# Attention scores of two maps in alternating products on separate row groups, for B and C two heads together in every other step

## The chip, the cores and the metric

The kernel runs on one core of one Trainium2 chip. The metric is the device time in microseconds (us) of one execution.

## What is computed

One inference step of a two-layer model with 128 context tokens and 512 latent tokens (640 together), width 1024. Each layer normalises, projects, runs four branches (A differential attention, B neighbourhood attention, C latent attention, D a convolution), gates and merges them, and ends in a mixture of experts. The change touches the scores of branches A, B and C only. Cut to what matters:

```
# A: 4 heads, two maps each, 32 columns a map; B and C: 4 heads each, one map of 64 columns
s = einsum('bqhmd,bkhmd->bhmqk', q, k) * scale          # A
w = softmax(s)[:, :, 0] - lam * softmax(s)[:, :, 1];  o = w @ v
p = softmax(q @ k.T * scale (+ bias and mask in B));  o = p @ v      # B, C
```

A latent token attends to 128 cached and 512 own keys (640), a context token to its own 128.

## The kernel before, in words

It is written engine by engine, with semaphores by hand. All products are made of fp16 halves: an fp32 operand is split in a high and a low part, and `passes` (L413) issues three matmuls, high by high, high by low, low by high, into one PSUM area.

Attention is one stage in each layer. Queries are taken in five tiles of 128 tokens: four latent tiles first, the context tile last (`ORDER`). A tile has twelve heads: 0 to 3 are A's with two maps each, 4 to 7 are B's, 8 to 11 C's, one map each, so 16 maps (`MAPS`). `head(g)` gives the tile, head and maps of the global head number g. Each engine walks over the steps g and does, in this order, a part for several heads:

- TensorE (L1036 to L1057): the scores of head g+1 (`score`), at tile boundaries six transposes of finished outputs (L1047), `turn` of head g-1 (five fp32 transposes of the weights into the PSUM area `pr(2)`, L1021), `values` of head g-2 (15 small matmuls), and then the step's share of the gate projection, in sets of three matmuls of 320 columns (`gate_set`): eight sets in steps whose next head is one of A's, four in the others (`quota`). The gate sets fill TensorE while the other engines work.
- ScalarE (L1480 to L1535): the scaled output of head g-3 (L1487), the exponentials of head g (L1502), the gate's tanh (L1414) where a gate tile has ended, the high half of the turned weights of head g-1 (L1524, "the cast"), and conversions of gate weights (L1341).
- VectorE (L2112 to L2180): the low half of the turned weights of head g-2 (L2117, "the subtraction"), then for head g+1 the bias (B alone, L2127) and the row maximum (L2130), then the reciprocal of head g's sums (L2145), for A the mixing of two maps (L2155). In the step of head g-2 = 5 it also takes the variance of A's outputs (L2164 to L2168), at g-2 = 7 it scales them (L2172 to L2177).

`pr(2)`, into which `turn` writes, is a single buffer: `turn` waits with `pt_ready` until the subtraction of the head before is done. A score goes to `pr(0)` or `pr(1)`, by the parity of its map (banks 0 and 1, or 2 and 3), and waits with `ex_ready` until the exponential two maps earlier has read it.

A's maps lie 32 rows apart in `qThi` and `kThi` (rows 0, 32, 64 or 96), B's and C's 64 rows apart (rows 0 or 64). A map's score is two pieces, of 128 and of 512 keys (`SEG`), with three matmuls each.

Of the kernel before, what the change touches and what calls it, by code (L numbers as in the profile page):

```python
# [16 lines left out]
P = 128  # L17
# [4 lines left out]
TOK = CTX + LAT  # L22
# [46 lines left out]
MAPS = 16  # L69
# [13 lines left out]
def build(nc, t):  # L83
    ctx = ExitStack()
    with ctx:
# [3 lines left out]
        def sig(name, per_layer=0, before=0):  # L89
            return Signal(ctx.enter_context(nc.semaphore(name)), per_layer, before)  # L90
# [62 lines left out]
        kThi = ab[:, AR:AR + 4608].rearrange("p (c k) -> p c k", c=6)  # L153
        kTlo = ab[:, AR + 4608:AR + 9216].rearrange("p (c k) -> p c k", c=6)
        vhi = ab[:, AR + 9216:AR + 13824].rearrange("p (c k) -> p c k", c=6)
        vlo = ab[:, AR + 13824:AR + 18432].rearrange("p (c k) -> p c k", c=6)
        qThi = ab[:, AR + 18432:AR + 22272].rearrange("p (c k) -> p c k", c=6)
        qTlo = ab[:, AR + 22272:AR + 26112].rearrange("p (c k) -> p c k", c=6)
# [116 lines left out]
        def pr(pair):  # L275
            return PS[:, pair, 384:1024]
# [3 lines left out]
        def bank(n, w=512):  # L280
            return PS[:, n // 2, 512 * (n % 2):512 * (n % 2) + w]
# [72 lines left out]
        s_done = sig("s_done", TILES * MAPS)  # L354
        mx_ready = sig("mx_ready", TILES * MAPS)
        ex_ready = sig("ex_ready", TILES * MAPS)
# [56 lines left out]
        def passes(pe, out, st_hi, st_lo, mv_hi, mv_lo, first, last):  # L413

            for n, (st, mv) in enumerate(((st_hi, mv_hi), (st_hi, mv_lo), (st_lo, mv_hi))):
                ins = pe.matmul(out, st, mv, start=first and n == 0, stop=last and n == 2)  # L416
            return ins

        def passes640(pe, pair, st_hi, st_lo, mv_hi, mv_lo, first, last):

            for n, (st, mv) in enumerate(((st_hi, mv_hi), (st_hi, mv_lo), (st_lo, mv_hi))):
                for a, b in SEG:
                    ins = pe.matmul(pr(pair)[:, a:b], st, mv[:, a:b], start=first and n == 0, stop=last and n == 2)  # L423
            return ins

        def ran_before(eng):


            b, ran = (eng.value_load(loopi[0:1, n:n + 1], min_val=0, max_val=LAYERS * (PAIRS + 1)) for n in (0, 2))
            return b, ran, b + ran  # L430
# [12 lines left out]
        def head(g):  # L443

            if not 0 <= g < HEADS_ALL:
                return None
            ti, hd = divmod(g, HDS)
            return ti, ORDER[ti], hd, ((2 * hd, 2 * hd + 1) if hd < 4 else (hd + 4,))
# [309 lines left out]
        def _(pe):  # L758

            pe.wait_ge(*consts_in(0, 5 * 16))  # L760
            for tile in range(TILES):
# [3 lines left out]
                for k in range(KC):  # L765
                    ins = pe.transpose(PS[:, tile % 4, k * P:(k + 1) * P], xtok[:, tile, k * P:(k + 1) * P], ident[:, :])
# [98 lines left out]
            for l in range(LAYERS):  # L865
# [3 lines left out]
                for u in range(2):  # L869
                    pe.wait_ge(*w_lo(l, V_IN + u + 1))  # L870
                    for c in range(2):
                        for k in range(KC):
                            if u == 0 and c == 0:
                                pe.wait_ge(*h_ready(l, k + 1))
                            w = slice(k * 256 + c * P, k * 256 + (c + 1) * P)
                            ins = passes640(pe, 2 * u + c, whi[u][:, w], wlo[u][:, w], hhi[:, k, :], hlo[:, k, :],
                                            k == 0, k == KC - 1)
                        ins.then_inc(du_done.sem, 1)

                for u in range(2, IN_UNITS):  # L880
                    n = 256 if u < IN_UNITS - 1 else 160
                    pe.wait_ge(*w_lo(l, V_IN + u + 1))
                    for tile in range(TILES):
                        g = (u - 2) * TILES + tile
                        if g == LN_MEAN:
# [3 lines left out]
                            for (a, b), z0 in zip(SEG, (0, CTX + PAD)):  # L889
                                for c in range(2):  # L890
                                    ins = pe.matmul(pr(0)[:, a:b], ones[:, :], zacc[:, c, z0:z0 + b - a],
                                                    start=c == 0, stop=c == 1)
                            ins.then_inc(mu_done.sem, 1)
                        if g == LN_VAR:

                            pe.wait_ge(*proj_ready(l, g - 2))
                            for c in range(2):
                                pe.wait_ge(*zsq_ready(l, c + 1))
                                for a, b in SEG:
                                    ins = pe.matmul(pr(2)[:, a:b], ones[:, :], zsg[:, c, a:b], start=c == 0, stop=c == 1)  # L900
# [9 lines left out]
                        for k in range(KC):  # L910
                            ins = passes(pe, bank(g % 6, n), hhi[:, k, tile * P:(tile + 1) * P],
                                         hlo[:, k, tile * P:(tile + 1) * P], whi[u % 2][:, k * n:(k + 1) * n],
                                         wlo[u % 2][:, k * n:(k + 1) * n], k == 0, k == KC - 1)
# [28 lines left out]
                for n in range(TILES + 2):  # L942
                    own = n < TILES
                    if n <= TILES:
# [5 lines left out]
                        for c in range(0 if own else 2, 3):  # L950
                            src = cn[:, c * P:(c + 1) * P] if own else cache[:, 1024:1152]
                            ins = pe.transpose(bank(0)[:, c * P:(c + 1) * P], src, ident[:, :])
# [6 lines left out]
                        for c in range(4):  # L959
                            ins = pe.transpose(bank(4 + 2 * (n % 2))[:, c * P:(c + 1) * P], src[:, c * P:(c + 1) * P],  # L960
                                               ident[:, :])
                        ins.then_inc(ab_t.sem, 1)
                    if own:
                        if n:
                            pe.wait_ge(*ab_ready(l, 2 * n))
                        for c in range(4):
                            ins = pe.transpose(bank(5)[:, c * P:(c + 1) * P],
                                               proj[:, n, C_BQ + c * P:C_BQ + (c + 1) * P], ident[:, :])
                        ins.then_inc(ab_t.sem, 1)
                    gate(2 * n)  # L970
                    if n:
# [4 lines left out]
                        for c in range(0 if n <= TILES else 2, 4):  # L976
                            ins = pe.transpose(bank(3)[:, c * P:(c + 1) * P], qkc[:, c * P:(c + 1) * P], ident[:, :])
# [14 lines left out]
                pe.wait_ge(*c_ready(l, 6))  # L992
                pe.wait_ge(*v_ready(l, 1))

                def score(ti, tile, m):

                    if ti or m >= 2:
                        pe.wait_ge(*ex_ready(l, ti * MAPS + m - 1))
                    if m < 8:
                        lo, n, c = 32 * (m % 4), 32, m // 4  # L1000
                    else:
                        lo, n, c = 64 * (m % 2), 64, (m - 8) // 2 + 2
                    q = (slice(lo, lo + n), c, slice(tile * P, (tile + 1) * P))
                    for a, b in SEG if tile else SEG[:1]:
                        k = (slice(lo, lo + n), c, slice(a, b) if tile else slice(TOK, TOK + P))
                        ins = passes(pe, pr(m % 2)[:, a:b], qThi[q], qTlo[q], kThi[k], kTlo[k], True, True)
                    ins.then_inc(s_done.sem, 1)

                def turn(ti, tile, hd):

# [13 lines left out]
                def values(ti, tile, hd):  # L1024

                    pe.wait_ge(*pt_ready(l, ti * HDS + hd + 1))
                    if ti or hd:
                        pe.wait_ge(*o_ready(l, ti * HDS + hd))
                    kts = range(TILES) if tile else (5,)
                    for c, kt in enumerate(kts):  # L1030
                        ins = passes(pe, bank(6, 64), pthi[:, hd % 2, c * P:(c + 1) * P],
                                     ptlo[:, hd % 2, c * P:(c + 1) * P], vhi[:, kt, hd * 64:(hd + 1) * 64],
                                     vlo[:, kt, hd * 64:(hd + 1) * 64], c == 0, c == len(kts) - 1)
                    ins.then_inc(pv_done.sem, 1)

                for g in range(-1, HEADS_ALL + 4):  # L1036
                    if head(g + 1):
                        for m in head(g + 1)[3]:
                            score(*head(g + 1)[:2], m)
                    if head(g - 4) and head(g - 4)[2] == HDS - 1:  # L1040

                        ti = head(g - 4)[0]
                        pe.wait_ge(*o_ready(l, (ti + 1) * HDS))
                        pe.wait_ge(*on_ready(l, ti + 1))
                        pe.wait_ge(*pt_ready(l, min(g - 1, HEADS_ALL)))
                        for c in range(6):
                            ins = pe.transpose(PS[:, 2, c * P:(c + 1) * P], otok[:, ti % 2, c * P:(c + 1) * P], ident[:, :])  # L1047
                        ins.then_inc(ot_done.sem, 1)
                    early = 4 if head(g - 4) and head(g - 4)[2] == HDS - 1 and head(g - 1) else 0
                    for i in GATE_SETS[g][:early]:  # L1050
                        gate_set(i)
                    if head(g - 1):
                        turn(*head(g - 1)[:3])
                    if head(g - 2):
                        values(*head(g - 2)[:3])
                    for i in GATE_SETS[g][early:]:
                        gate_set(i)  # L1057

# [4 lines left out]
                for d in range(KC):  # L1063
                    for n, b in enumerate(SLOTS):
# [13 lines left out]
                        for k in range(2):  # L1078
                            w = slice(d * P, (d + 1) * P)
                            ins = passes640(pe, n, wohi[:, b, k, w], wolo[:, b, k, w], bhi[k], blo[k], k == 0, k == 1)  # L1080
# [3 lines left out]
                for u in range(OUT_UNITS):  # L1084
                    pe.wait_ge(*w_lo(l, V_OUT + u + 1))
                    for c in range(2):
                        d = 2 * u + c
                        pe.wait_ge(*x1_ready(l, d - 1))
                        for k in range(KC):
                            if d == 0:  # L1090
# [3 lines left out]
                            ins = passes640(pe, c, whi[u % 2][:, w], wlo[u % 2][:, w], mhi[:, k, :], mlo[:, k, :],  # L1094
                                            k == 0, k == KC - 1)
# [8 lines left out]
                for k in range(KC):  # L1104
                    pe.wait_ge(*hf_ready(l, KC + k + 1))
                    pe.wait_ge(*wr_in(l, 4 * 16))
                    for a, b in SEG:
                        ins = pe.matmul(pr(2)[0:20, a:b], wr[:, k, :], hf[:, k % 2, a:b], start=k == 0, stop=k == KC - 1)
                    if k >= 2:
                        pe.wait_ge(*htk_ready(l, k - 1))  # L1110
                    for tile in range(TILES):
                        ins = pe.transpose(pr(k % 2)[:, tile * P:(tile + 1) * P], hf[:, k % 2, tile * P:(tile + 1) * P],
                                           ident[:, :])
                    ins.then_inc(hf_used.sem, 1)
                pe.wait_ge(*lg_ready(l, 1))
                for tile in range(TILES):
                    ins = pe.matmul(bank(4)[:, tile * 20:(tile + 1) * 20], lgT[:, tile * P:(tile + 1) * P],
                                    ident[0:20, 0:20], start=True, stop=True)
# [13 lines left out]
                for n in range(10):  # L1132
                    ins = pe.matmul(bank(5)[:, 0:CHUNKS + 2], rowhot[:, n, :], chhot[:, n, :], start=n == 0, stop=n == 9)
# [7 lines left out]
                b, ran, past = ran_before(pe)  # L1141
# [53 lines left out]
                with pe.Fori(0, p + 1) as i:  # L1195
                    for n in range(2):

                        c, j = i * 2 + (1 + n), 1 - n
# [1352 lines left out]
```

## Time and profile before

| what | value |
|---|---|
| median of 3 runs | 1963.04 us (1955.48 to 1973.32) |
| the profiled execution's own time | 1951.89 us |
| its span, first to last instruction | 1950.0 us |
| TensorE busy | 1724.3 us, 88% |
| VectorE, ScalarE, GpSimd busy | 1149.6, 936.8, 439.9 us |
| mean granted TensorE clock | 0.93 |
| attention in the first layer | from 305 to 589 us of the span |

The second layer's attention runs from about 1247 to 1531 us. "Busy" is the time in which an engine had an instruction in work; the granted clock is a share of 2.4 GHz.

### The profile page before, as it was taken

To read this page: it belongs to the slowest core of one execution; us is meant where nothing else is said; L and a number is where in the kernel's file an instruction comes from. 1 tells how busy PE (TensorE), PEld (TensorE's weight loads), DVE (VectorE), ACT (ScalarE), POOL (GpSimd) and SP (SyncE) were. 2 spreads that over 40 slices of the span, in tenths; PEclk is the share of its full clock that TensorE was granted. 3 is DMA by queue.
4 is the path that set the end of the run, shared out by engine and by line. 5 is a ranking of instruction groups with operands and counts; after the bars stand their busy time and mean duration, and the time that the engine had idled before them with its cause. 6 is when DMAs were issued, how large, how long until landed. Compare 5 with 4: busy or idle time off the path is not lost.

```text
span 1950.0 us, 34375 instructions
## 1 busy us (share of the span) xinstructions
PE 1724.3 (88%) x13375; PEld 1136.0 (58%) x13375; DVE 1149.6 (59%) x1736; ACT 936.8 (48%) x1530; POOL 439.9 (23%) x298
## 2 busy tenths in 40 slices
PE   6799889999999986888789998999999999479876
PEld 4378766666665543444466876666666556234436
DVE  4595365666427336787766825466662661677854
ACT  3322545666651123777532244566665221357753
POOL 0032251111131201333202324211112130023312
PEclk7899999999999986999869998999999999689995
DMA  8554236422237355999745523222214631389964
GB/s 290 177 195 165 75 137 208 147 88 72 93 120 244 118 216 191 331 397 383 258 152 171 191 75 100 82 96 68 68 54 131 224 110 50 145 306 384 389 245 162
DMA packets 189433, 346.44 MB, mean 178 GB/s; under 512 B 14894, under 2 KB 98031, under 8 KB 189295
## 3 DMA queue, kind: packets, MB, share of 16 engines
q1 hardware_dynamic: 179975, 315.31, 46.2%
q0 software_dynamic: 7776, 28.32, 3.8%
q8 instruction: 98, 1.61, 0.3%
q10 hardware_dynamic: 1543, 0.88, 0.2%
q14 instruction: 41, 0.33, 0.1%
HBM read 283.48 MB, written 60.98 MB: 177 GB/s over the span
## 4 chain that ended last, share of the span: by engine, by line
PE 64%; issue 11%; DVE 9%; DMA 8%; ACT 5%; DVEq 1%; POOLq 1%; POOL 1%; SPq 1%; ACTq 0%
PE PS L416 41%; PE PS L423 9%; DMA wf<-in_moe_w 4%; PE PS L1021 4%; DMA arena<-in_moe_w 2%; PE PS L827 2%; PE PS L785 1%; DMA hpart<-h_rows,wulo 1%; PE PS L809 1%; DVE arena L2243 1%; DVE scratch L1817 1%; DVE hpart L1835 1%; DVE scratch L2214 1%; DMA hpart<-y_rows,wulo 1%; ACT whi L1569 1%
## 5 line engine op out<-in xcount | busy, mean ns | idle before, releaser
L1672 POOL TENSOR_TENSOR wlo<-wf,whi 128x1024 f16<-128x1024 f32 x112 | 251.8, 2268 | 957.3 <-ACT whi L1341 957.3
L416 PE MATMUL PS<-hpart,whi 128*128 128x320 f16 x2048 | 424.2, 300 | 10.1 <-ACT arena L1414 8.5
L416 PE MATMUL PS<-hpart,wlo 128*128 128x320 f16 x1024 | 307.0, 300 | 0.0
L416 PE MATMUL PS<-whi,hpart 128*128 128x256 f16 (+2 forms) x1568 | 297.4, 290 | 8.5 <-DVE hpart L2396 4.9
L416 PEld LDWEIGHTS PS<-hpart,whi 128*128 128x128 f16 x2048 | 192.5, 98 | 85.3 <-issue 16.5
L416 PE MATMUL PS<-wlo,hpart 128*128 128x256 f16 (+2 forms) x784 | 225.4, 290 | 0.0
L2130 DVE TENSOR_REDUCE stat<-PS 128x1 f32<-128x640 f32 (+1 forms) x160 | 111.1, 715 | 158.4 <-PE PS L416 156.1
L416 PEld LDWEIGHTS PS<-whi,hpart 128*128 128x128 f16 x1568 | 151.6, 98 | 66.9 <-issue 25.4
L2243 DVE TENSOR_TENSOR arena<-arena 128x2048 f16<-128x2048 f32 x66 | 149.5, 2287 | 40.2 <-ACT arena L1569 40.1
L416 PE MATMUL PS<-arena 128*128 128x64 f16 (+4 forms) x2376 | 170.2, 228 | 0.0
L1414 ACT ACTIVATE arena<-PS,pcol 128x320 f32<-128x320 f32 x128 | 67.4, 527 | 161.1 <-PE PS L416 156.7
L1966 DVE SCALAR_TENSOR_TENSOR scratch<-scratch,cw 128x655 f32<-128x655 f32 x120 | 138.8, 1198 | 4.8 <-issue 0.4
L1569 ACT CAST arena<-arena 128x2048 f16<-128x2048 f32 x66 | 123.5, 1897 | 24.6 <-DMA arena<-in_moe_w 24.6
L416 PEld LDWEIGHTS PS<-arena 128*128 128x128 f16 (+2 forms) x2376 | 108.0, 97 | 40.9 <-issue 17.4
L1341 ACT CAST whi<-wf 128x1024 f16<-128x1024 f32 (+1 forms) x84 | 110.5, 1315 | 44.3 <-PE PS L423 44.3
L416 PEld LDWEIGHTS PS<-hpart,wlo 128*128 128x128 f16 x1024 | 100.5, 98 | 39.6
L1524 ACT CAST arena<-PS 128x640 f16<-128x640 f32 (+1 forms) x120 | 72.6, 605 | 101.4 <-PE PS L1021 101.4
L1502 ACT ACTIVATE scratch<-PS,stat 128x640 f32<-128x640 f32 (+1 forms) x160 | 113.0, 713 | 6.7 <-DVE stat L2130 5.0
L2117 DVE TENSOR_TENSOR arena<-PS,arena 128x640 f16<-128x640 f32 (+1 forms) x120 | 85.5, 712 | 32.6 <-ACT arena L1524 31.9
L416 PE MATMUL PS<-arena,hpart 128*128 128x512 f16 x384 | 97.5, 408 | 4.8 <-issue 4.7
L2243 DVE TENSOR_TENSOR wlo<-wf,whi 128x2048 f16<-128x2048 f32 x36 | 82.2, 2289 | 28.7 <-ACT whi L1569 27.1
L1379 ACT COPY arena<-PS 128x256 f32<-128x256 f32 (+1 forms) x80 | 28.8, 361 | 144.9 <-PE PS L416 144.9
(331 smaller groups left out, 2845.1 us busy)
## 6 DMA issues: line engine op xcount, KB each, us to landing
arena<-in_moe_w SPq DMA_DIRECT2D x66, 1024.0 KB, 8.3
arena<-in_w_ada SPq DMA_DIRECT2D x40, 1024.0 KB, 8.0
wf<-in_moe_w SPq DMA_DIRECT2D x36, 1024.0 KB, 9.1
wf<-in_w_gate SPq DMA_DIRECT2D x32, 1024.0 KB, 5.5
g_rows<-arena SPq DMA_DIRECT2D x128, 160.0 KB, 1.8
wf<-in_w_in SPq DMA_DIRECT2D x18, 1024.0 KB, 7.8
y_rows<-scratch SPq DMA_DIRECT2D x34, 512.0 KB, 9.1
arena<-g_rows SPq DMA_DIRECT2D x24, 640.0 KB, 5.2
```

What stands on the lines that cost most here:

```text
L416: ins = pe.matmul(out, st, mv, start=first and n == 0, stop=last and n == 2)
L423: ins = pe.matmul(pr(pair)[:, a:b], st, mv[:, a:b], start=first and n == 0, stop=last and n == 2)
L1021: ins = pe.transpose(pr(2)[:, c * P:(c + 1) * P], src[:, c * P:(c + 1) * P], ident[:, :])
L1341: return act.copy(whi[j][:, a:b] if dst is None else dst, wf[j][:, a:b])
L1502: act.activation(ex[:, m % 4, 0:nk], pr(m % 2)[:, 0:nk], ACT.Exp, bias=stat[:, 0, m:m + 1], accum_out=stat[:, 1, m:m + 1]).then_inc(ex_rea ...
L1524: act.copy(pthi[:, hd % 2, 0:nk], pr(2)[:, 0:nk]).then_inc(pt_hi.sem, 1)
L1569: act.copy(mwhi[3 * j + q], mwf[3 * j + q]).then_inc(mw_hi.sem, 1)
L1672: ins = pool.tensor_tensor(lo[:, a:b], wf[j][:, a:b], hi[:, a:b], ALU.subtract)
L1966: ins = dve.scalar_tensor_tensor(out=zacc[:, c, :], in0=zpad[:, c, k:k + NZ], scalar=cw[:, c, k:k + 1], in1=zacc[:, c, :], op0=ALU.mult, o ...
L2117: dve.tensor_tensor(ptlo[:, hd % 2, 0:nk], pr(2)[:, 0:nk], pthi[:, hd % 2, 0:nk], ALU.subtract).then_inc(pt_ready.sem, 1)
L2130: dve.tensor_reduce(stat[:, 0, m:m + 1], pr(m % 2)[:, 0:nk], AX_X, ALU.max, negate=True).then_inc(mx_ready.sem, 1)
L2243: dve.tensor_tensor(mwlo[3 * j + q], mwf[3 * j + q], mwhi[3 * j + q], ALU.subtract).then_inc((mw_lo2 if q == 2 else mw_lo).sem, 1)
```

## The change

The scores of maps m and m+1 (an even m) are issued by one call. For each piece and each of the three passes it issues the matmul of one map and then that of the other. The pair waits until all earlier exponentials are done, and both maps are signalled together on the last matmul. For A the two maps belong to one head, as before. For B and C they belong to two heads, so that a pair is made at heads 4, 6, 8 and 10, and steps whose next head is 5, 7, 9 or 11 have no scores. The pairs of heads 1 to 4 stand at the start of the step, as before; those of heads 0, 6, 8 and 10 stand behind `turn` and `values`, ahead of the gate sets. The other engines' programs are unchanged.

```diff
-                def score(ti, tile, m):
-
-                    if ti or m >= 2:
-                        pe.wait_ge(*ex_ready(l, ti * MAPS + m - 1))
-                    if m < 8:
-                        lo, n, c = 32 * (m % 4), 32, m // 4
-                    else:
-                        lo, n, c = 64 * (m % 2), 64, (m - 8) // 2 + 2
-                    q = (slice(lo, lo + n), c, slice(tile * P, (tile + 1) * P))
+                def scores(ti, tile, hd, ms):
+
+                    ms = (ms[0], ms[0] + 1)
+                    if ti or ms[0]:
+                        pe.wait_ge(*ex_ready(l, ti * MAPS + ms[0]))
+                    part = []
+                    for m in ms:
+                        lo, n, c = (32 * (m % 4), 32, m // 4) if m < 8 else (64 * (m % 2), 64, (m - 8) // 2 + 2)
+                        part.append((slice(lo, lo + n), c))
                     for a, b in SEG if tile else SEG[:1]:
-                        k = (slice(lo, lo + n), c, slice(a, b) if tile else slice(TOK, TOK + P))
-                        ins = passes(pe, pr(m % 2)[:, a:b], qThi[q], qTlo[q], kThi[k], kTlo[k], True, True)
-                    ins.then_inc(s_done.sem, 1)
+                        for n in range(3):
+                            for m, (rows, c) in zip(ms, part):
+                                q = (rows, c, slice(tile * P, (tile + 1) * P))
+                                k = (rows, c, slice(a, b) if tile else slice(TOK, TOK + P))
+                                ins = pe.matmul(pr(m % 2)[:, a:b], (qThi, qThi, qTlo)[n][q], (kThi, kTlo, kThi)[n][k],
+                                                start=n == 0, stop=n == 2)
+                    ins.then_inc(s_done.sem, 2)
...
                 for g in range(-1, HEADS_ALL + 4):
-                    if head(g + 1):
-                        for m in head(g + 1)[3]:
-                            score(*head(g + 1)[:2], m)
+                    pair = head(g + 1) and (head(g + 1)[2] < 4 or head(g + 1)[2] % 2 == 0)
+                    if pair and 1 <= head(g + 1)[2] <= 4:
+                        scores(*head(g + 1))
...
                     if head(g - 2):
                         values(*head(g - 2)[:3])
+                    if pair and not 1 <= head(g + 1)[2] <= 4:
+                        scores(*head(g + 1))
                     for i in GATE_SETS[g][early:]:
                         gate_set(i)
```

## Rows read from the trace of the kernel before

**Rows 1.** The page: busy time and share, then busy tenths in 40 slices.

```profile
PE 1724.3 (88%) x13375; PEld 1136.0 (58%) x13375; DVE 1149.6 (59%) x1736; ACT 936.8 (48%) x1530; POOL 439.9 (23%) x298
...
PE   6799889999999986888789998999999999479876
...
PEclk7899999999999986999869998999999999689995
```

**Rows 2.** Busy time by stretch: the second latent tile, and the context tile.

```profile
354.00:407.00 53.00, 52.28 (x536) 36.15 (x536) 32.73 (x59) 34.90 (x72) 8.73 (x5) 1.00 0.42 145
...
513.00:589.00 76.00, 71.81 (x594) 50.20 (x589) 24.88 (x63) 39.76 (x94) 21.70 (x11) 1.00 0.35 118
```

**Rows 3.** Timeline of TensorE, from `turn` of head 2 in the second tile.

```profile
379.57 0.74 PE L1021 MATMUL PS<-ident,scratch 128*128 128x128 f32 x5 [0.34 <-DVE arena L2137]
...
382.04 0.74 PE L1021 MATMUL PS<-ident,scratch 128*128 128x128 f32 x5 [0.37 <-DVE arena L2117]
...
385.69 0.77 PE L1021 MATMUL PS<-ident,scratch 128*128 128x128 f32 x5
...
389.38 0.77 PE L1021 MATMUL PS<-ident,scratch 128*128 128x128 f32 x5
389.98 0.60 PE L416 MATMUL PS<-arena 128*128 128x64 f16 x15
...
390.41 0.43 PE L416 MATMUL PS<-hpart,whi 128*128 128x320 f16 x2
...
391.64 0.43 PE L416 MATMUL PS<-hpart,whi 128*128 128x320 f16 x2
...
392.14 0.99 PE L416 MATMUL PS<-arena 64*128 64x128 f16 x6
393.06 0.77 PE L1021 MATMUL PS<-ident,scratch 128*128 128x128 f32 x5
...
400.42 0.77 PE L1021 MATMUL PS<-ident,scratch 128*128 128x128 f32 x5
...
408.01 0.77 PE L1021 MATMUL PS<-ident,scratch 128*128 128x128 f32 x5
...
412.41 1.11 PE L416 MATMUL PS<-arena 32*128 32x128 f16 x12
413.45 0.77 PE L1021 MATMUL PS<-ident,scratch 128*128 128x128 f32 x5
```

**Rows 4.** Timeline of VectorE over the same steps.

```profile
381.07 0.82 DVE L2117 TENSOR_TENSOR arena<-PS,arena 128x640 f16<-128x640 f32 x1 [0.30 <-ACT arena L1524]
...
389.48 0.70 DVE L2127 TENSOR_TENSOR PS<-PS,bias 128x512 f32<-128x512 f32 x1 [1.29 <-PE PS L416]
...
391.07 0.81 DVE L2117 TENSOR_TENSOR arena<-PS,arena 128x640 f16<-128x640 f32 x1
393.16 0.82 DVE L2130 TENSOR_REDUCE stat<-PS 128x1 f32<-128x640 f32 x1 [1.29 <-PE PS L416]
...
393.98 0.40 DVE L2164 TENSOR_TENSOR scratch<-arena 128x256 f32<-128x256 f32 x1
...
395.03 0.82 DVE L2117 TENSOR_TENSOR arena<-PS,arena 128x640 f16<-128x640 f32 x1
...
401.33 0.16 DVE L2172 RECIPROCAL ostat<-ostat 128x4 f32<-128x4 f32 x1
...
402.41 0.82 DVE L2117 TENSOR_TENSOR arena<-PS,arena 128x640 f16<-128x640 f32 x1
```

**Rows 5.** Timeline of ScalarE: a cast of turned weights, and a table load.

```profile
380.35 0.69 ACT L1524 CAST arena<-PS 128x640 f16<-128x640 f32 x1 [1.91 <-PE PS L1021]
...
396.50 1.28 ACT L1510 ACT_TABLE_LOAD   x1
```

**Rows 6.** Busy time by stretch, in the stage ahead of the attention.

```profile
240.00:260.00 20.00, 17.74 (x138) 13.69 (x137) 11.21 (x26) 11.40 (x28) 12.99 (x15) 1.00 0.26 85
260.00:280.00 20.00, 16.84 (x118) 12.78 (x117) 13.16 (x32) 8.55 (x26) 8.46 (x8) 0.91 0.47 159
```

## The prediction

> **What bounds the kernel now.** I read the page first: TensorE is busy for 88% of the span and the slices of the attention stand at 9 or close to it, with the granted clock at full speed [rows 1]. Then the busy time by stretch: in a latent tile of the attention TensorE is busy for 52.28 of 53 us, VectorE for 32.73, ScalarE for 34.90; in the context tile for 71.81 of 76 [rows 2]. So here each microsecond taken off TensorE shows in the time, as long as TensorE does not have to wait instead. Whether it does, a share cannot say; for that I read the timelines of the three engines over one tile and follow one chain through them.
>
> One head of B or C takes a step of 3.68 us on TensorE [rows 3]: `turn` 0.60 (389.38 to 389.98), `values` 0.43 (to 390.41), four gate sets of 0.41 (the last starts at 391.64), then the score. The last set leaves off at 391.64 + 0.41 = 392.05 and the score starts at 392.14: 0.09 for going from 128 rows to 64. The score holds the engine for 0.92 (392.14 to 393.06). Sum 0.60 + 0.43 + 1.64 + 0.09 + 0.92 = 3.68. In A the twelve matmuls of two maps hold it for 1.04 (412.41 to 413.45) in a step of 5.44 (408.01 to 413.45).
>
> The second chain runs beside it: `turn` (single buffer), ScalarE's cast, VectorE's subtraction, next `turn`. At the tile boundary it decides already: `turn` at 379.57, cast at 380.35, subtraction at 381.07, next `turn` at 382.04, with TensorE idle for 0.37 before it [rows 3 to 5]. That is 2.47 us, its shortest period, and 0.97 of it lie from the start of the subtraction to the `turn`.
>
> **What the matmuls themselves give back.** The number of matmuls stays; what changes is how many run side by side. In A they already do: two maps of six matmuls each take 1.04 where one map of B takes 0.92, so the second lags by 0.12. Alternation can take away at most that: I take 0.11 a pair (bounds 0 and 0.12). For B and C no row shows two halves of 64 rows together. The bounds are 0.92, as if the second map cost nothing, and 2 x 0.92 = 1.84. A's row is the nearest, the only one with two row groups at work, so I take 0.92 + 0.02 = 0.94. One row switch of 0.09 goes too. So a B or C pair gives back 2 x (0.92 + 0.09) - (0.94 + 0.09) = 0.99, a tile 4 x 0.99 + 4 x 0.11 = 4.4 us, eight latent tiles 35 us. That is the gain if nothing else were late.
>
> The Trainium skill (TensorE: Matmul & The Clock Gate, Part 3, Packing small matmuls) says that matmuls start and end strictly in program order. By that rule A's second map could not begin before the first map's last matmul, a pair would have cost 2 x 0.92 less one last matmul of 512 columns, an estimate near 1.6 us, and alternation would save about 0.7 x 32 = 22 us in A alone. The row of 1.04 for both maps speaks against it: what the rule would give is already in the time of before [rows 3].
>
> **What is late next.** The score was also cover. VectorE works in order, and in a step it takes the maximum of head g+1 before the subtraction of head g-1. A pair that stands behind `turn` and `values` makes VectorE wait for it; behind the pair only four gate sets (1.64) stand before the next `turn`, which needs that subtraction. From the start S of the pair:
>
> - the first VectorE instruction starts at S + 1.04 (before 392.14 to 393.16 = 1.02; the second map adds 0.02) [rows 3, 4];
> - heads 6 and 7: bias, maximum and reciprocal 1.59 (389.48 to 391.07), then 0.97 to the next `turn`: S + 3.60;
> - heads 8 and 9: maximum and reciprocal 0.82 (393.16 to 393.98), the variance 1.05 (to 395.03), 0.97: S + 3.88;
> - heads 10 and 11: 0.82, then the scaling of A's outputs 1.08 (401.33 to 402.41), 0.97: S + 3.91.
>
> TensorE is ready at S + 0.94 + 1.64 = S + 2.58 each time: it stands for 1.02, 1.30 and 1.33. S lies 0.60 + 0.43 + 0.09 = 1.12 behind the `turn` ahead of it. The step after has no score: 0.60 + 0.43 + 1.64 = 2.67, just over the chain's 2.47, no stall.
>
> Now the tile from `turn` to `turn`, before [rows 3] and after:
>
> - head 2 to 3: 2.47 and 2.47. Here the gate sets stand ahead of `turn`, so the chain sets the end; the score of head 5, gone from this step, only lengthens the wait.
> - 3 to 4: 3.65 and 2.67, so -0.98.
> - 4 to 6: 7.37, and 1.12 + 3.60 + 2.67 = 7.39, so +0.02.
> - 6 to 8: 7.36, and 1.12 + 3.88 + 2.67 = 7.67, so +0.31.
> - 8 to 10: 7.59 (with head 0's pair in it), and 1.12 + 3.91 + 2.67 = 7.70, so +0.11.
> - 10 to 11: 5.44. Now head 0's pair stands behind `values` here and head 1's ahead of `turn`: 1.12 + 0.93 + 8 x 0.41 + 0.09 + 0.93 = 6.35, so +0.91. No stall behind head 0's pair: eight sets (3.28) cover it.
> - 11 to 0 and 0 to 1: 5.44 less 0.11 each, so -0.22.
> - 1 to 2, across the boundary: +0.02.
>
> Sum +0.17 a tile: 4.4 gained, nearly 4.6 waited. To it comes the stricter wait of a pair for both earlier exponentials. It bites at most at heads 8 to 10, where ScalarE also loads two tables of 1.28 [rows 5]: I take 0.1, bounds 0 and 0.5. Eight tiles: 8 x 0.27 = +2.2 us. The context tile's steps hold eight gate sets and are set by gates; a pair of short scores saves at most 0.3 there and I take -0.3 in all, bounds -2 and +1. That both maps are signalled together costs A 0.02 at most: the maximum of the first map started behind all twelve matmuls before. DMA queues and GpSimd are passed by nothing: they wait for the gate tiles, which move with the tile by tenths.
>
> Sum +1.9: 1951.89 + 1.9 = 1953.8 for the profiled execution. The median lies 11.15 above that execution, so 1963.04 + 1.9 = about 1965.
>
> The Trainium skill (TensorEngine Tiling (Array Packing), PSUM Bottleneck) warns that tiling speeds up TensorE but not the emptying of PSUM, which may then bound. As a matter of throughput the trace does not agree: VectorE's work for two heads of B is about 2 x (1.59 + 0.81) = 4.8 us of 7.37, and the 35 us would be had. It is the order of the work, not its amount, that takes them back.
>
> **The rivals.**
>
> A. Slower: the two halves of 64 rows do not run side by side when they alternate. A pair then costs 1.84 instead of 0.94. S + 1.84 + 1.64 = S + 3.48 on TensorE, and the first maximum starts 0.90 later too, so the whole 0.9 lands on the path: 8 tiles x 4 pairs x 0.9 = +29, about 1994. For it: no row shows that order. Against it: A's 1.04. It decides from a pair of about 1.5 us on. Chance 0.08.
>
> B. Faster: the late pair does not hold up `turn`. If the subtraction came in time for the `turn` behind each late pair, 1.02 + 1.30 + 1.33 = 3.65 a tile would go, 8 x 3.65 = 29: about 1936. For it: the cast and the subtraction need nothing of the new pair. Against it: VectorE takes them in order, and the rows show the subtraction directly behind the maximum. Half of it, with my waits read too long, would give 1950. Chance for over 1% faster 0.05.
>
> C. The clock: with stalls of about 1.3 us in every other step TensorE's busy share in these steps falls from 98% to near 85%, and the clock could fall to 1.2 GHz. Ahead of the attention a stretch with 17.74 of 20 us busy kept 1.00, the next with 16.84 of 20 had 0.91 [rows 6]; the gaps there are single long ones, mine would be short. Where it fell for a tenth of the 8 x 30 us of B and C, those 24 us would stretch by half to nearly double: +12 to +20, about 1980. Chance 0.06.
>
> **How the numbers follow.** My forecast 1965 has 0.81: its own errors are tenths of a us in some 50 places, within 10 us either way. A has 0.08, C 0.06 (about half of it above 1%), B 0.05. A run of this kernel can tell about 1% (20 us) from no change. Faster by more than 1% 0.07 (B, and a little of my own error), slower by more 0.13 (A, half of C, the rest), within it 0.80. The range of 8 in 10 takes half of the way to B and most of that to A: 1948 to 1984.
>
> **What the profile after should show.** The six-by-two matmuls of B in about 1.0 us, followed by gate sets; in A a pair of 0.93 instead of 1.04. TensorE's busy time in a latent tile lower by about 4 us and its idle time higher by as much, put down to VectorE's subtraction (L2117), before `turn`; a latent tile of 53.1 to 53.3 us instead of 52.92; both layers alike; the clock at 1.00. A tile of 56 or more would mean A, one below 51 B, a granted clock below 1.00 C.

## The result, and the profile after

The changed kernel is slower: 2013.62 us median against 1963.15, the ratio 1.0236 with a 95% interval of 1.0203 to 1.027. My 1965 and the range up to 1984 were wrong. A second, later measurement (experiment 8) gave 1.024 (1.0192 to 1.0288).

The page of the kernel after, busy time and the slices of TensorE and its clock, to be read against [rows 1]:

```profile
span 2013.4 us, 34375 instructions
...
PE 1707.2 (85%) x13375; PEld 1132.1 (56%) x13375; DVE 1176.7 (58%) x1736; ACT 937.7 (47%) x1530; POOL 438.0 (22%) x298
...
PE   6799889888889986888779998988889999568885
...
PEclk7899999999999986999859998999999999679996
```

TensorE's busy time fell by 17 us while the span grew by 63. VectorE's grew by 27, although it still has 1736 instructions.

Next the busy time by stretch: one latent tile (360 to 418 us; from the first `turn` of this tile to that of the next it is 57.9 us, before 52.92), and four microseconds in it.

```profile
360.00:418.00 58.00, 49.44 (x537) 35.41 (x536) 36.17 (x59) 35.22 (x72) 8.95 (x4) 0.97 0.39 133
413.00:417.00 4.00, 3.18 (x26) 2.65 (x27) 2.30 (x4) 1.74 (x4) 0.00 (x0) 0.57 0.00 0
```

Against [rows 2]: TensorE's busy time per tile is 2.8 us less, VectorE's 3.4 more, and the clock, 1.00 before, is 0.97, and 0.57 in the stretch from 413 to 417. The place shows on TensorE's timeline over the same heads as [rows 3], where L1025 is `turn`, L1009 the pair of scores and L1051 the six transposes at the tile boundary:

```profile
381.26 0.99 PE L1009 MATMUL PS<-arena 64*128 64x128 f16 x12
382.18 0.55 PE L1051 MATMUL PS<-ident,arena 128*128 128x128 f32 x3
...
385.02 0.74 PE L1025 MATMUL PS<-ident,scratch 128*128 128x128 f32 x5 [0.34 <-DVE arena L2143]
...
387.49 0.74 PE L1025 MATMUL PS<-ident,scratch 128*128 128x128 f32 x5 [1.29 <-DVE arena L2123]
...
390.13 0.71 PE L1025 MATMUL PS<-ident,scratch 128*128 128x128 f32 x5
...
391.21 0.99 PE L1009 MATMUL PS<-arena 64*128 64x128 f16 x12
394.78 0.74 PE L1025 MATMUL PS<-ident,scratch 128*128 128x128 f32 x5 [0.85 <-DVE arena L2123]
...
402.37 0.74 PE L1025 MATMUL PS<-ident,scratch 128*128 128x128 f32 x5 [1.15 <-DVE arena L2123]
...
405.01 0.71 PE L1025 MATMUL PS<-ident,scratch 128*128 128x128 f32 x5
...
406.31 0.99 PE L1009 MATMUL PS<-arena 64*128 64x128 f16 x12
413.82 1.30 PE L1025 MATMUL PS<-ident,scratch 128*128 128x128 f32 x5 [4.79 <-DVE arena L2123]
```

Twelve matmuls of a pair of B last 0.99 us, as long as the six of one map before [rows 3]. The waits of 0.85 and 1.15 us behind late pairs are the ones forecast. The wait of 4.79 us is not. VectorE in the same step:

```profile
407.34 0.82 DVE L2136 TENSOR_REDUCE stat<-PS 128x1 f32<-128x640 f32 x1 [2.64 <-PE PS L1009]
...
408.15 0.16 DVE L2178 RECIPROCAL ostat<-ostat 128x4 f32<-128x4 f32 x1
408.38 2.30 DVE L2180 TENSOR_TENSOR arena<-arena,ostat 128x256 f32<-128x256 f32 x1
410.75 2.19 DVE L2183 TENSOR_TENSOR arena<-arena,rowg 128x256 f32<-128x256 f32 x1
412.86 0.81 DVE L2123 TENSOR_TENSOR arena<-PS,arena 128x640 f16<-128x640 f32 x1
```

and GpSimd, whose one work here is the subtraction that gives the low half of the gate weights (two pieces, merged in one row):

```profile
408.28 4.38 POOL L1678 TENSOR_TENSOR wlo<-wf,whi 128x1024 f16<-128x1024 f32 x2 [24.33 <-ACT whi L1347]
```

The scaling of A's outputs, two multiplications of 0.42 us each before (the block from 401.33 to 402.41 in [rows 4]), takes 2.30 and 2.19 us, and begins 0.1 us behind GpSimd's work. The second multiplication ends 0.3 us behind GpSimd's end at 412.66. In the kernel before GpSimd began only once the scaling was done (its first multiplication began at 401.57, 1.45 us ahead of GpSimd):

```profile
403.02 4.22 POOL L1672 TENSOR_TENSOR wlo<-wf,whi 128x1024 f16<-128x1024 f32 x2 [24.66 <-ACT whi L1341]
```

Here are the periods from `turn` to `turn` between heads 2 and 11 of the second latent tile, from the starts of `turn` in each trace. The columns "forecast" and "after" are to be compared; the last two belong to experiments 3 and 6.

| heads | before | forecast | after | conversion later | subtraction first |
|---|---|---|---|---|---|
| 2 to 3 | 2.47 | 2.47 | 2.47 | 2.47 | 2.47 |
| 3 to 4 | 3.65 | 2.67 | 2.64 | 2.64 | 2.64 |
| 4 to 6 | 7.37 | 7.39 | 7.29 | 7.29 | 6.36 |
| 6 to 8 | 7.36 | 7.67 | 7.59 | 7.59 | 7.14 |
| 8 to 9 | 3.78 | 5.03 | 8.81 | 5.17 | 4.03 |
| 9 to 10 | 3.81 | 2.67 | 4.04 | 2.64 | 2.61 |
| 10 to 11 | 5.44 | 6.35 | 6.28 | 6.28 | 6.28 |

All agree within 0.1 us, but for two: 8 to 9, where the scaling lies, is 3.8 us too long, and 9 to 10, behind it, 1.4 us. The step 8 to 9 takes 8.80 or 8.81 us in each of the eight latent tiles. The attention of a layer takes 304.1 and 304.9 us instead of 284.0, so 41 us of the loss are in these stages. In this profiled execution the stages between the two attentions also took 20 us more (experiment 8).

### The profile page after: what moved, and what is told of

Same layout as the page of the kernel before. It is cut to its first block, busy times and chain, and to the rows that moved or that the text cites. A ratio compares the mean times of both kernels' runs of the same rounds, so it can differ in the third digit from the quotient of the medians.

```text
span 2013.4 us, 34375 instructions
## 1 busy us (share of the span) xinstructions
PE 1707.2 (85%) x13375; PEld 1132.1 (56%) x13375; DVE 1176.7 (58%) x1736; ACT 937.7 (47%) x1530; POOL 438.0 (22%) x298
## 4 chain that ended last, share of the span: by engine, by line
PE 57%; DVE 13%; issue 11%; DMA 8%; ACT 6%; DVEq 1%; POOLq 1%; SPq 1%; POOL 1%; another core or an unknown queue 0%; ACTq 0%
PE PS L416 32%; PE PS L423 9%; DMA arena<-in_moe_w 3%; PE PS L1025 3%; PE PS L1009 3%; DMA wf<-in_moe_w 3%; PE PS L827 2%; PE PS L785 1%; DVE arena L2123 1%; DVE stat L2136 1%; DMA hpart<-h_rows,wulo 1%; DVE arena L2180 1%; PE PS L809 1%; DVE arena L2183 1%; DVE arena L2249 1%
## 5 line engine op out<-in xcount | busy, mean ns | idle before, releaser
L416 PE MATMUL PS<-hpart,whi 128*128 128x320 f16 x2048 | 430.3, 303 | 14.3 <-ACT arena L1420 14.0
L1025 PE MATMUL PS<-ident,scratch 128*128 128x128 f32 x504 | 81.7, 289 | 66.9 <-DVE arena L2123 64.2
L2123 DVE TENSOR_TENSOR arena<-PS,arena 128x640 f16<-128x640 f32 (+1 forms) x120 | 85.4, 712 | 52.3 <-ACT arena L1530 50.9
L1025 PEld LDWEIGHTS PS<-ident,scratch 128*128 128x128 f32 x504 | 59.4, 146 | 90.5 <-issue 73.6
```

What stands on the lines that cost most here:

```text
L1025: ins = pe.transpose(pr(2)[:, c * P:(c + 1) * P], src[:, c * P:(c + 1) * P], ident[:, :])
L2123: dve.tensor_tensor(ptlo[:, hd % 2, 0:nk], pr(2)[:, 0:nk], pthi[:, hd % 2, 0:nk], ALU.subtract).then_inc(pt_ready.sem, 1)
```

## The experiments

I had two theories. Theory P: VectorE's multiplications, whose two inputs both lie in SBUF, and GpSimd's subtraction shut each other out, and the late pair moved the one into the other. Rival Q: they are slow for a reason of the new place itself. Beside these a rival on the clock.

**1. The scaling ahead of the late pair's maximum.** The kernel after, VectorE alone changed:

```diff
                         dve.tensor_tensor(ptlo[:, hd % 2, 0:nk], pr(2)[:, 0:nk], pthi[:, hd % 2, 0:nk], ALU.subtract
                                           ).then_inc(pt_ready.sem, 1)
+                    if head(g - 2) and head(g - 2)[2] == 7:
+                        ti, _, hd, _ = head(g - 2)
+                        oa = otok[:, ti % 2, 0:256].rearrange("p (h n) -> p h n", h=4)
+                        dve.wait_ge(*ostd_ready(l, ti + 1))
...
-                    if head(g - 2) and head(g - 2)[2] in (5, 7):
+                    if head(g - 2) and head(g - 2)[2] == 5:
```

> Kernel after, but VectorE scales A's outputs (two multiplications, 128x256, both inputs in SBUF) ahead of the maximum in the same step, while it waits for the late pair, and so before GpSimd begins its subtraction of gate weights. Theory P (the two multiplications and GpSimd's subtraction shut each other out; in the kernel after they meet in each latent tile): the multiplications take 0.42 us each instead of 2.30 and 2.19, turn 8 to turn 9 falls from 8.81 to about 3.95 us, the clock no longer falls there, the tile takes about 51.7 instead of 58.0 us: 8 x 6.3 = 50 us less, near the kernel before (ratio to before 0.99 to 1.00). Rival Q (the multiplications are slow wherever a late pair stands, for a reason of their own): they stay above 2 us, the time stays near 2013. Rival R (the clock falls because of the many short stalls, not because of the one long wait): the step shrinks, but the granted clock still falls once in each tile.

Measured: 1949.2 us, ratio to before 0.9956 (0.9924 to 0.9987). Turn 8 to turn 9 takes 4.09 us, 9 to 10 2.64, a latent tile 51.8 us. No fall of the clock is left in the attention. VectorE's and GpSimd's timelines:

```profile
401.95 0.42 DVE L2131 TENSOR_TENSOR arena<-arena,ostat 128x256 f32<-128x256 f32 x1
402.45 0.43 DVE L2134 TENSOR_TENSOR arena<-arena,rowg 128x256 f32<-128x256 f32 x1
```

```profile
405.37 4.22 POOL L1678 TENSOR_TENSOR wlo<-wf,whi 128x1024 f16<-128x1024 f32 x2 [24.31 <-ACT whi L1347]
```

The tile is 6.1 us shorter than in the kernel after, near the 6.3 that P said. Q, read as "beside any late pair", falls; as "behind the late pair's maximum" it is still open. R falls: waits of about a microsecond are as frequent as in the kernel after, and the clock stays up.

**2. The kernel before, with the scaling one step later.** No pair, no late score:

```diff
-                    if head(g - 2) and head(g - 2)[2] in (5, 7):
+                    if head(g - 2) and head(g - 2)[2] in (5, 8):
```

> Kernel before, with VectorE's scaling of A's outputs moved one step later, into the stretch in which GpSimd subtracts gate weights (403.0 to 407.2 us in the second tile). Nothing else is changed. Theory P: at least one of the two multiplications takes about 2 us instead of 0.42, the subtraction behind it comes late, each latent tile is 1 to 2 us longer than 52.92, 8 to 16 us in all. Rival Q (the place of the late pair makes them slow, not GpSimd): 0.42 us each and no difference that can be measured.

Measured: 1962.64 us, ratio 1.0033 (0.9999 to 1.0066). Its timelines:

```profile
405.91 2.17 DVE L2174 TENSOR_TENSOR arena<-arena,ostat 128x256 f32<-128x256 f32 x1
408.16 0.43 DVE L2177 TENSOR_TENSOR arena<-arena,rowg 128x256 f32<-128x256 f32 x1
```

```profile
403.58 4.22 POOL L1672 TENSOR_TENSOR wlo<-wf,whi 128x1024 f16<-128x1024 f32 x2 [24.65 <-ACT whi L1341]
```

The first multiplication, begun inside GpSimd's second piece, ends 0.3 us behind it (403.58 + 4.22 = 407.80, the multiplication 408.08). The second, begun when GpSimd was done, takes 0.43. The attention of a layer grows from 284.0 to 288.2 us, 8.4 us in all. The ratio of the measured times, +6.5 us, agrees; its interval begins at 0.9999, so by itself it hardly tells this from nothing. So the slowness can be made without the change, which Q excluded.

**3. The kernel after, with GpSimd's work begun later.** TensorE's and VectorE's programs stay as they are. ScalarE converts gate weights one step later where they fall in head 9's step, and GpSimd waits for that:

```diff
-                    for n in done:
-                        gate_cast(n)
+                    if g == 0:
+                        kept = []
+                    kept = kept + list(done)
+                    if not (head(g) and head(g)[2] == 9):
+                        for n in kept:
+                            gate_cast(n)
+                        kept = []
```

> Kernel after with nothing moved on TensorE or VectorE: ScalarE converts the gate weights one step later where they fall in the step of head 9, so that GpSimd's subtraction begins some 3 us later. The scaling of A's outputs stays behind the late pair's maximum. Theory P: its multiplications take 0.42 us each, turn 8 to turn 9 takes 5.0 us (my forecast for it) instead of 8.81, the clock stays up, a latent tile takes about 52.8 us and the time is that of the kernel before within 0.5%. Rival Q (the place behind the late pair makes them slow): still about 2.2 us each and 2010 in all.

Measured: 1954.35 us, ratio 0.9986 (0.9962 to 1.001). VectorE's timeline, to be held against that of the kernel after, with the multiplications in the same place behind the maximum, and GpSimd's:

```profile
403.05 0.82 DVE L2141 TENSOR_REDUCE stat<-PS 128x1 f32<-128x640 f32 x1 [2.64 <-PE PS L1009]
...
404.09 0.42 DVE L2185 TENSOR_TENSOR arena<-arena,ostat 128x256 f32<-128x256 f32 x1
404.59 0.42 DVE L2188 TENSOR_TENSOR arena<-arena,rowg 128x256 f32<-128x256 f32 x1
```

```profile
408.38 4.22 POOL L1683 TENSOR_TENSOR wlo<-wf,whi 128x1024 f16<-128x1024 f32 x2 [28.73 <-ACT whi L1347]
```

This settles P against Q: the same two multiplications in the same place of VectorE's program are slow or not with GpSimd's time alone. It is also the kernel of my forecast: its attention takes 284.0 and 284.3 us a layer against 284.0 before, and the column "conversion later" of the table follows the forecast within 0.15 us.

**4. The alternation alone undone.** The kernel after with the map loop outermost:

```diff
-                    for a, b in SEG if tile else SEG[:1]:
-                        for n in range(3):
-                            for m, (rows, c) in zip(ms, part):
+                    for m, (rows, c) in zip(ms, part):
+                        for a, b in SEG if tile else SEG[:1]:
+                            for n in range(3):
```

> Kernel after with the alternation undone alone: the same pairs at the same places, but all six matmuls of one map, then all six of the other. Theory X (maps on separate row groups run side by side whatever the order in the program): a pair of B or C holds TensorE for 1.04 us as A's did before, instead of 0.92; a step with one of them is 0.1 us longer, 8 x 8 x 0.1 = about 6 us in all, less where VectorE is waited for. Rival Y (for 64 rows only alternation lets them run together): a pair holds it for about 1.8 us and the time is 25 to 55 us above the kernel after.

Measured: 2015.38 us, ratio 1.0308 (1.0262 to 1.0354), beside 2001.5 of the kernel after on the same chip. A pair of B on TensorE's timeline:

```profile
393.00 1.12 PE L1009 MATMUL PS<-arena 64*128 64x128 f16 x12
```

1.12 us instead of 0.99, and steps with a late pair of 4.77 and 5.07 instead of 4.65 and 4.95: 0.12 us, X holds and Y falls. Two halves of 64 rows run side by side in either order; alternation is worth 0.12 us a pair. The whole difference, 14 us, is more than the 6 us expected. The attention takes 5.8 and 6.3 us more a layer than in experiment 8; part of that is the clock, which in every second latent tile stays low for longer (9 to 10 takes 5.09 instead of 4.2 us there).

**5. All pairs ahead of `turn`.**

```diff
-                    if pair and 1 <= head(g + 1)[2] <= 4:
+                    if pair:
                         scores(*head(g + 1))
...
-                    if pair and not 1 <= head(g + 1)[2] <= 4:
-                        scores(*head(g + 1))
```

> Kernel after, but every pair stands ahead of turn, as the scores did before. Theory P: the scaling of A's outputs begins 1.4 us ahead of the end of the weight conversion, as before, and does not meet GpSimd; the multiplications take 0.42 us each; what is left is my chain of waits, with a tile of 51.9 to 52.9 us (the pair now waits for the second exponential): ratio to before 0.995 to 1.00. Rival Q (pairs for B and C are bad for the tile wherever they stand): 55 us a tile or more, the time stays above 1985.

Measured: 1958.45 us, ratio 1.0006 (0.9979 to 1.0033), at the upper end of the range of P. The multiplications take 0.43 us each, and Q falls: the second and third latent tile take 52.1 and 53.4 us. What ate the gain is another wait, of which I had named the place but not the size: TensorE's rows at the pair of heads 10 and 11, in the first latent tile,

```profile
346.01 1.12 PE L1009 MATMUL PS<-arena 64*128 64x128 f16 x12 [2.24 <-ACT scratch L1506]
347.07 1.33 PE L1025 MATMUL PS<-ident,scratch 128*128 128x128 f32 x5
```

show 2.24 us for the second exponential of the pair before, for which ScalarE's two table loads (1.28 us each) stand in line. The wait comes in every latent tile, and the step takes 5.97 us, here 6.10. `turn` behind it lasts 1.33 instead of 0.74, because the clock fell (0.59 on average from 346 to 350 us). It did so in the first and third latent tile of each layer, not in the others.

**6. The subtraction first.** The kernel after, VectorE alone changed: in steps with a late pair of B or C it takes the variance or scaling (now in `scale_outputs`) and the subtraction of the head just turned ahead of the pair's maximum. So it takes away the waits and, as experiment 1 did, the meeting with GpSimd.

```diff
-                    if head(g - 2):
-                        ti, tile, hd, ms = head(g - 2)
-                        nk = TOK if tile else P
-                        dve.wait_ge(*pt_hi(l, g - 1))
...
+                    late = head(g + 1) and head(g + 1)[2] in (6, 8, 10)
+                    subs = ([] if head(g) and head(g)[2] in (6, 8, 10) else [g - 2]) + ([g - 1] if late else [])
+                    for q in subs:
+                        if q == g - 1:
+                            scale_outputs(g)
+                        if head(q):
+                            ti, tile, hd, ms = head(q)
+                            nk = TOK if tile else P
+                            dve.wait_ge(*pt_hi(l, q + 1))
```

> Kernel after, but in the steps with a late pair of B or C (next head 6, 8, 10) VectorE first takes the scaling or the variance of A's outputs and the subtraction of the head turned in this step, and only then the maximum of the late pair. So turn no longer waits behind that maximum. Theory S (the stalls of 1.0 to 1.3 us behind each late pair come from VectorE's order alone): turn to turn over a late pair falls from 4.65 and 4.95 to about 3.70 us, a latent tile to about 49.3 us, 8 x 3.6 = 29 us less than before: about 1934, ratio 0.985. Rival T (the cast on ScalarE or the next exponentials are late next): 4.2 us or more per such step, ratio 0.99 to 1.0.

Measured: 1935.67 us, ratio 0.9891 (0.9839 to 0.9943). It is faster than both kernels, and 13.5 us below experiment 1, which moves the scaling alone; the attention takes 273.7 us a layer instead of 284.0. Two late pairs on TensorE's timeline:

```profile
382.81 0.99 PE L1009 MATMUL PS<-arena 64*128 64x128 f16 x12
385.37 0.71 PE L1025 MATMUL PS<-ident,scratch 128*128 128x128 f32 x5
...
395.23 0.74 PE L1025 MATMUL PS<-ident,scratch 128*128 128x128 f32 x5 [0.69 <-DVE arena L2151]
...
396.70 0.99 PE L1009 MATMUL PS<-arena 64*128 64x128 f16 x12 [0.29 <-ACT scratch L1508]
```

Behind the pair at 382.81 there is no wait. Steps with a late pair take 3.64 and 3.67 us, as S said; the third takes 4.03 and the one ahead of it 3.47, where a cast and an exponential stand behind ScalarE's two table loads. So what T named bites at one pair of three, if less than the 4.2 us that it asked for, and the tile is 50.3 us, not 49.3.

**7. More gate sets in the gaps that are left.** Experiment 6 with

```diff
-                return 8 if (g + 1) % HDS < 4 else 4
+                return 8 if (g + 1) % HDS < 4 or g >= HDS and (g + 1) % HDS in (4, 11) else 4
```

> Kernel e5 with eight instead of four gate sets in two steps of each of the last three latent tiles and of the context tile's share before it (next head 4, where TensorE still stands 1.4 us for VectorE's subtraction, and next head 11). 24 to 32 sets leave the gate-bound steps of the context tile. Theory: a latent tile grows by 1.8 us (1.64 in the step that has no stall, 0.2 in the other), the context tile loses three or four halves of 4.13 us: 6 to 9 us a layer less, ratio to before 0.980 to 0.985. Rival (the tail without gate sets is bound by the chain of the other engines or by GpSimd's gate weights, and gives nothing back): 0.989 or more.

Measured: 1943.77 us, ratio 0.9932 (0.9908 to 0.9955): above the 0.980 to 0.985 of the theory. It is not told apart from experiment 6, whose interval overlaps, and a layer's attention is as long as there within 0.7 us. From the context tile's first `turn` to the end of the stage it takes 54.5 us instead of 66.9, so 12.4 us did come back, three halves of 4.13, and the rival's reason is not it. But what lies ahead of that `turn` grew by 12.7 and 11.8 us in the two layers instead of 5.5. The shifted gate tiles shift GpSimd's work too, and in the second latent tile it meets the scaling again:

```profile
396.05 0.42 DVE L2135 TENSOR_TENSOR arena<-arena,ostat 128x256 f32<-128x256 f32 x1
396.55 2.19 DVE L2138 TENSOR_TENSOR arena<-arena,rowg 128x256 f32<-128x256 f32 x1
```

Around it TensorE stands for 1.11 us (for the subtraction ahead of it) and, 1.2 us later, for 1.24 us (for an exponential), and the clock falls (0.72 on average from 396 to 402 us), in both layers. In the third latent tile of the first layer GpSimd meets the mixing of A's maps instead: they begin 0.03 us apart, and the mixing takes 2.85 us instead of 0.88.

**8. The kernel after once more**, for the 20 us between the first and the second attention. Nothing was edited.

> The kernel after, once more. 41.6 us of its profiled execution's excess lie in the two attention stages and about 20 us in the first layer's stages behind the attention. Theory V (those 20 us are the spread of single executions, as in the kernel before, whose runs lie up to 18 us apart): the stages behind the first attention take about 942 us to the end of the second attention less its own excess, and the ratio comes nearer to 1.021. Rival W (the change lengthens them too): about 20 us again.

Measured: 2001.5 us, ratio 1.024, and a profiled span of 1994.2 us. From the end of the first attention to the first score of the second it took 657.9 us; the kernel before took 657.7, the first execution of the kernel after 678.0, the other experiments 660 to 662. The attention took 304.7 us in both layers. So the 20 us are no part of what the change does, and W falls. That they were the spread of single executions, as V says, is not shown: the three executions measured beside the first profile lie 1 to 11 us below it, and there is no trace of them. The ratio did not come down to 1.021, but its interval holds it.

## Why the prediction was wrong

**The step that failed** is the third line of the chain behind the late pair, that of heads 10 and 11: "0.82, then the scaling of A's outputs 1.08". The 1.08 was the row of before, and I moved it to a later time without asking who else is at work then; of GpSimd I had only said that nothing passes it and that it waits for the gate tiles. ScalarE's conversion of gate weights starts GpSimd. Before, the scaling's first multiplication began 1.45 us ahead of GpSimd; the late maximum put it 0.10 us behind. There reciprocal and multiplications took 4.71 us (408.15 to 412.86) instead of 1.08: 3.63 us, the same as 8.81 - 5.17 = 3.64 between the kernel after and experiment 3. Eight latent tiles make 29 us.

**The clock** was the other part. With TensorE waiting 4.79 us it fell each time, and `turn` 9 to 10 took 3.9 to 4.3 us instead of 2.64: 8 x 1.5 = 12 us. Together 41 us, which is what the attention stages lost. Rival C had the clock fall through many short waits. In experiments 1, 3 and 6 these did nothing; here one long wait did it. Two short ones close together can do it as well, as experiment 7 shows.

The Trainium skill (SBUF — State Buffer, Who interferes with whom) states this: an instruction of VectorE with both inputs in SBUF contends with one of GpSimd that reads SBUF, and the contention is an exclusive lock. The rows agree: 0.42 us became 1.83 to 2.30 where a multiplication of the scaling began inside a piece of GpSimd's, and it ended 0.3 us behind the end of that piece. I had not weighed this rule, though it spoke against moving such instructions of VectorE without a look at GpSimd. The trace of before held a case as well, the square of A's outputs (L2164), whose line I read only for its usual 0.40:

```profile
L2164 DVE TENSOR_TENSOR scratch<-arena x5: 403/406/1631, 341.1 to 548.6; 128x256 f32<-128x256 f32 x5
```

Of its five in the first layer (minimum, median, maximum in ns) one took 1.63 us, in the context tile.

The rows show the other side too: with a lead it is VectorE that keeps its time. The mixing of A's maps also reads two tiles of SBUF, and here it begins 0.39 us ahead of GpSimd:

```profile
378.99 0.89 DVE L2161 SCALAR_TENSOR_TENSOR scratch<-scratch,cfa 128x640 f32<-128x640 f32 x1
```

```profile
379.38 4.57 POOL L1678 TENSOR_TENSOR wlo<-wf,whi 128x1024 f16<-128x1024 f32 x2 [24.52 <-ACT whi L1347]
```

The mixing takes its usual 0.89; it is GpSimd's first piece that takes 2.48 us instead of 2.12, ending 1.99 us behind the mixing's end. It is so in all eight latent tiles of the kernels before and after (in the kernel before the piece takes 2.34 us).

**What was right.** The pair at 0.94: it holds TensorE for 0.92 (381.26 to 382.18), and two maps of 64 rows run side by side, so rival A fell. Its sign, a tile of 56 us or more, did come, from another cause; the length of the pair tells the two apart. The waits behind the late pairs and their cause, VectorE's order: experiment 6 takes them away by that order alone. The sum of the tile without the collision: experiment 3 has 52.9 us against the 53.1 to 53.3 of the forecast, and its 1954.35 against 1958.01 is "no change", as forecast. The step from `turn` 2 to 3, where no gain was to come, did not move.

**What was misplaced.** The stricter wait for both exponentials, taken as 0.1 us, is 2.24 us with the pairs in front (experiment 5); in the kernel after, behind `turn` and `values`, it does not show. And I gave 0.13 to "slower" with two mechanisms. The pairs side by side were not lost, and the clock fell, but through a wait that rival C did not have; the meeting with GpSimd was in no rival.

The excess of 50 us in the first measurement (interval 40 to 53) and of 47 in the second (38 to 56) is not told apart from the 41 us in the attention.

## What to carry to other kernels

When a change delays instructions on VectorE that read two tiles of SBUF, look at what GpSimd does at their new time, not only at the chain on VectorE; a duration of before holds only beside the same neighbours. A score, a gate set or any other work is also cover: count what stands between a signal and the next wait on each engine after the move. And when engines that work in order feed a single buffer, serve that buffer's release before the newest product. Here the scaling put ahead of the maximum turned +2.4% into -0.4% (experiment 1), and the subtraction with it made -1.1% (experiment 6).

## What the runs showed of the hardware that I had not expected

- A multiplication of 128x256 on VectorE took 1.83 to 2.30 us where it began 0.1 to 0.6 us behind the start of a piece of GpSimd's subtraction and 0.42 alone. Each one begun inside a piece, early or late (the square of A's outputs began 0.8 to 1.1 us behind its start), ended 0.28 us behind the piece's end. Instructions with an input in PSUM (the subtraction L2123, the maximum) kept their 0.80 to 0.83 us beside GpSimd.
- Where VectorE's instruction with two inputs in SBUF began 0.4 to 0.5 us first, it kept its 0.88 us and GpSimd's piece took 2.34 (before) or 2.48 us (after) instead of 2.12. With a lead of 0.03 us it took 2.85 (experiment 7).
- Two maps on separate row groups ran side by side whatever the order of their matmuls: they held TensorE for 1.04 to 1.05 us when one map was issued after the other, 0.92 alternating, for 32 and for 64 rows.
- In the attention the granted clock fell to 1.2 GHz at each wait of TensorE of 4.7 to 4.8 us and at one of 2.24 us in four cases of eight (experiment 5). It stayed at 2.4 GHz with single waits of 0.7 to 1.3 us, several in a tile, but fell where two of 1.11 and 1.24 us stood 1.2 us apart (experiment 7, in both layers).
